# One expert's token gather in a mixture-of-experts step: tokens as the moving operand, 512 columns at a time, then transposed

## The chip, the cores and the metric

The kernel runs on one core of a Trainium2 chip. The metric is the device time of one execution in microseconds (us); the time before is the median of three runs. Engines are named as in the profile: PE is TensorE's matmuls and PEld its weight loads, DVE is VectorE, ACT is ScalarE, POOL is GpSimd, SP is the sync engine that issues the weight transfers.

## What is computed

One inference step of a two-layer decoder for 256 prompt tokens and 8 sample tokens (264 in all, width 1024). The last part, and the one that the change touches, is a mixture of 8 experts, each with an inner width of 3584; each token goes to its best two:

```python
logits = (h @ w_router).astype(jnp.float32) + b_router.astype(jnp.float32)
top_v, top_i = lax.top_k(logits, TOP_K)
gates = jax.nn.softmax(top_v, axis=-1)
...
for e in range(N_EXPERTS):
    y = (jax.nn.silu(h @ w1[e]) * (h @ w3[e])) @ w2[e]
    out = out + dense_gate[..., e:e + 1] * y
```

## The kernel before

Everything is float32 in memory. For the large products each operand is split into a high part, rounded to the format that PE streams quickly (F32R), and the remainder. A product is then three matmuls (`three`, L429 to L434): high by high, remainder by high, high by remainder.

**Weights.** An expert's weights come in 42 slabs of 1 MB (`eslabs`), through a ring of seven places filled by SP. For each slab ACT copies the high part (`high`, L1072, tile w_hi) and DVE subtracts it from the original (`low`, L1555, tile w_lo). There are three places for such pairs (`PAIRS`). ACT may write a place only when PE has used the slab that was in it three slabs before (semaphore `pair_used`); SP may refill a place of the ring only when DVE has made the remainder. The slabs of a chunk j of 512 inner channels are two of w1, two of w3, and two of w2 for the chunk before. The last two slabs of an expert are those of w2 for the last chunk, j = 6.

**An expert on PE** (`expert`): for each chunk, `product(1, j, 3)` and `product(3, j, 4)` multiply the gathered tokens (tiles xe_hi, xe_lo; 1024 channels in 8 blocks of 128, 128 token places) by w1 and w3, 24 matmuls of 512 columns each, 12 a slab. `turn(j)` transposes the activated product with four PE transposes (L814) into bank 5, ACT copies its high part (`turned_high`, L1086), DVE makes the remainder (`turned_low`, L1576), which sets `upT_ready`. `down(j)` then multiplies by w2 into banks 6 and 7, 12 matmuls a slab. `combine` scatters the former expert's result back by a matmul (L789), spread over the first chunks of the next expert.

**The gather** (`gather`, L771): for the next expert, while this one ends. `disp` holds 0/1 (which token goes to which of the 128 places), in three parts of 128, 128 and 8 tokens. For each of the 8 channel blocks of 128, the token rows (htok_hi, htok_lo) are the stationary operand and the 128 columns of disp stream: 8 blocks x 3 token parts x 2 (high, remainder) = 48 matmuls. The result in banks 0 and 1 has channels on partitions, as the products want it. Three more transposes (L777) turn the gated matrix. ACT copies the high part of both banks (`gathered_high`, L1077), DVE makes the remainder (`gathered_low`, L1560) and sets `xe_ready`, on which the next expert's first product waits.

**Order.** It is written out by hand for each engine, and each engine runs its list in order. PE at an expert's end: down(5), turn(6), gather, down(6), then the next expert's product(1, 0). In the program of ACT and of DVE one step of the loop over `eslabs` belongs to one slab k; it begins with `high` or `low` of slab k + 3, so with a wait for PE's use of slab k. In the step of (2, 5, 1) there follow turned_high or turned_low for chunk 6, and then gathered_high or gathered_low. The steps (2, 6, 0) and (2, 6, 1) hold only high or low. After the last step ACT copies half of the expert's result (L1103) and DVE the other half (L1601).

The first expert's gather has nothing around it; the next seven are issued in the expert before. The last expert issues none.

Of the kernel before, what the change touches and what calls it, by code (L numbers as in the profile page):

```python
# [9 lines left out]
ACT = mybir.ActivationFunctionType  # L10
# [66 lines left out]
def yoco_step(nc, w, o):  # L77
# [23 lines left out]
    with ExitStack() as ctx:  # L101
# [16 lines left out]
        def sem(name):  # L118
            return ctx.enter_context(nc.semaphore(name))
# [45 lines left out]
        def at(offset, *shape):  # L165
# [74 lines left out]
        ye = at(5632, D)  # L240
        disp = over("disp", "phase", 6656, [P, 3, SLOTS], F32R)
        dispg = at(7040, 3, SLOTS)
        comb = at(7424, NT)
        lg = at(7688, 3, NE)
        sel = at(7712, 3, NE)
# [47 lines left out]
        moe_ready, flag_ready = sem("moe_ready"), sem("flag_ready")  # L293
        route_built, gathered, comb_turned, comb_copied = (sem(n) for n in (
            "route_built", "gathered", "comb_turned", "comb_copied"))
        silu_done, up_ready, up_turned = (sem(n) for n in ("silu_done", "up_ready", "up_turned"))
        y0_copied, y1_copied, c_summed, y_added = (sem(n) for n in ("y0_copied", "y1_copied", "c_summed", "y_added"))
        y_turned, y_taken = sem("y_turned"), sem("y_taken")
# [127 lines left out]
        def _(pe):  # L426
# [331 lines left out]
            def gather(e, c, ahead):  # L758

                pe.wait_ge(route_built, e + (c * NE + ahead + 1))  # L760
                if ahead:

                    pe.wait_ge(y_added, e * KC + KC * (c * (NE + 1) + 1))
                elif c:
                    pe.wait_ge(y_added, KC * c * (NE + 1))
                pe.wait_ge(comb_copied, e + (c * (NE + 1) + ahead + 1))
                for k in range(KC):
                    for q in range(3):
                        n = rows[q]
                        for part, last in ((htok_hi, False), (htok_lo, q == 2)):  # L770
                            mm = pe.matmul(bank[k // 4][:, P * (k % 4):P * (k % 4) + SLOTS], part[0:n, q, P * k:P * (k + 1)], disp[0:n, q, :],  # L771
                                           start=(q == 0 and part is htok_hi), stop=last)
                    if k % 4 == 3:
                        mm.then_inc(gathered, 1)
                for q in range(3):
                    n = rows[q]
                    mm = pe.transpose(bank[2][0:SLOTS, P * q:P * q + n], dispg[0:n, q, :], ident[0:n, 0:n])  # L777
                mm.then_inc(comb_turned, 1)

            def combine(e, c, blocks=range(KC)):  # L780

# [10 lines left out]
            def expert(e, c, last):  # L792
# [21 lines left out]
                        mm = pe.transpose(bank[5][:, SLOTS * i:SLOTS * (i + 1)], up[0:SLOTS, P * i:P * (i + 1)], ident[0:SLOTS, 0:SLOTS])  # L814
                    mm.then_inc(up_turned, 1)

                def down(j):
                    pe.wait_ge(upT_ready, count(FCH, j + 2))
                    if j == 0:
                        pe.wait_ge(y0_copied, count(1, 1))  # L820
                        pe.wait_ge(y1_copied, count(1, 1))
                    for half in range(2):
                        hi, lo = weights(2, j, half, 2)
                        for i in range(2):
                            for q in range(2):
                                cols = slice(512 * q, 512 * (q + 1))
                                mm = three(bank[6 + q][0:SLOTS, :], (upT_hi[:, 2 * half + i, :], upT_lo[:, 2 * half + i, :]),
                                           (hi[:, i, cols], lo[:, i, cols]), j == 0 and half == 0 and i == 0, j == FCH - 1 and half == 1 and i == 1)
                        mm.then_inc(pair_used, 1)
# [15 lines left out]
                turn(FCH - 1)  # L845
                if not last:
                    gather(e, c, 1)
                down(FCH - 1)

            def experts(c):  # L850
                gather(0, c, 0)
                with pe.Fori(0, NE - 1) as e:
                    expert(e, c, False)
                expert(NE - 1, c, True)
                combine(NE, c)
# [18 lines left out]
        def _(act):  # L874
# [191 lines left out]
            def high(e, c, k):  # L1066
# [4 lines left out]
                    before_experts[slot] + 16 * ((c * NE + ahead) * len(use[slot]) + use[slot].index(k % PER_E) + 1)))  # L1071
                act.activation(w_hi[:, (NSPLIT + k) % PAIRS, :], ring[:, slot, :], ACT.Copy).then_inc(hi_done, 1)  # L1072

            def gathered_high(e, c, ahead):
                act.wait_ge(gathered, e * 2 + (2 * (c * NE + ahead) + 2))
                for q in range(2):
                    ins = act.activation(xe_hi[:, 4 * q:4 * q + 4, :], bank[q][:, :].rearrange("p (k n) -> p k n", k=4), ACT.Copy)  # L1077
                ins.then_inc(xe_hi_ready, 1)

            def expert(e, c, last):  # L1080
                def count(per, k):
                    return e * per + (c * NE * per + k)

                def turned_high(j):
                    act.wait_ge(up_turned, count(FCH, j + 1))
                    act.activation(upT_hi[:, :, :], bank[5][:, :].rearrange("p (k n) -> p k n", k=4), ACT.Copy).then_inc(upT_hi_ready, 1)  # L1086

                for k, (m, j, half) in enumerate(eslabs):

                    if k + PAIRS < PER_E or not last:  # L1090
                        high(e, c, k + PAIRS)
                    if (m, half) == (1, 1):
                        act.wait_ge(pair_used, used_by(e, c, 1, j))
                        act.wait_ge(up_ready, count(FCH, j + 1))
                        act.activation(up_s[0:SLOTS, :], bank[3][0:SLOTS, :], ACT.Silu).then_inc(silu_done, 1)
                        if j >= 1:
                            turned_high(j - 1)
                    if (m, j, half) == (2, FCH - 2, 1):
                        turned_high(FCH - 1)
                        if not last:  # L1100
                            gathered_high(e, c, 1)
                act.wait_ge(pair_used, used_by(e, c, 2, FCH - 1))
                act.activation(ye[0:SLOTS, 0:512], bank[6][0:SLOTS, :], ACT.Copy).then_inc(y0_copied, 1)  # L1103

            def experts(c):
                for k in range(PAIRS):
                    high(0, c, k)
                gathered_high(0, c, 0)
                with act.Fori(0, NE - 1) as e:
                    expert(e, c, False)  # L1110
                expert(NE - 1, c, True)
# [19 lines left out]
        def _(dve):  # L1131
# [420 lines left out]
            def low(e, c, k):  # L1552
                i, slot = (NSPLIT + k) % PAIRS, (NPRE + k) % RING
                dve.wait_ge(hi_done, e * PER_E + (NSPLIT + c * NE * PER_E + k + 1))
                dve.tensor_tensor(w_lo[:, i, :], ring[:, slot, :], w_hi[:, i, :].bitcast(F32), ALU.subtract).then_inc(lo_done, 1)  # L1555

            def gathered_low(e, c, ahead):
                dve.wait_ge(xe_hi_ready, e + (c * NE + ahead + 1))
                for q in range(2):
# [10 lines left out]
            def expert(e, c, last):  # L1570
# [8 lines left out]
                for k, (m, j, half) in enumerate(eslabs):  # L1579
# [16 lines left out]
                    if (m, j, half) == (2, FCH - 2, 1):  # L1596
                        turned_low(FCH - 1)
                        if not last:
                            gathered_low(e, c, 1)
                dve.wait_ge(pair_used, used_by(e, c, 2, FCH - 1))  # L1600
                dve.tensor_copy(ye[0:SLOTS, 512:1024], bank[7][0:SLOTS, :]).then_inc(y1_copied, 1)  # L1601

            def experts(c):
                route(0, c, 0)
                for k in range(PAIRS):
                    low(0, c, k)
                gathered_low(0, c, 0)
                with dve.Fori(0, NE - 1) as e:
                    expert(e, c, False)
# [119 lines left out]
```

## Time and profile before

| | |
|---|---|
| time before, median of 3 runs | 2040.87 us (2030.43 to 2042.6) |
| span of the profiled execution | 2030.6 us |
| PE busy | 1851.2 us, 91% |
| PEld busy | 1484.2 us, 73% |
| DVE busy | 1449.0 us, 71% |
| ACT busy | 1064.2 us, 52% |
| read from memory | 492 MB |
| mean granted TensorE clock | 0.889 |

The profiled execution's span is 0.2 us above the fastest of the three runs. Its total time is not told apart from its span. The experts run from 909 us to 2000 us. A matmul's duration in the trace includes its way through a pipeline, so that two neighbours overlap; what one costs PE is the distance from its start to the next one's. The granted clock is a share of full speed: 1.00 is 2.4 GHz and 0.50 is 1.2 GHz.

### The profile page before, as it was taken

What the parts mean: (1) busy time and instruction counts of PE and PEld (TensorE: products, weight loads), DVE (VectorE), ACT (ScalarE), POOL (GpSimd) and SP (SyncE); (2) the same over time, 40 slices, a digit from 0 to 9 for tenths busy, and PEclk for the clock granted to TensorE, in tenths of its full rate; (3) what the DMA queues carried; (4) which work ended last, traced back from release to release, by engine and by line L of the source; (5) the groups of instructions that cost most, each with busy time, mean ns of one, the idle gap of its engine ahead of it and who ended that gap; (6) DMA issues with size and microseconds to landing.
All of it is one profiled execution on the core that took longest, in us unless ns stands there. A gap on an engine that the chain in (4) does not pass through costs nothing.

```text
span 2030.6 us, 24253 instructions
## 1 busy us (share of the span) xinstructions
PE 1851.2 (91%) x9104; PEld 1484.2 (73%) x9104; DVE 1449.0 (71%) x1369; ACT 1064.2 (52%) x918; POOL 155.4 (8%) x113
## 2 busy tenths in 40 slices
PE   6567999788978999779999999999999999999995
PEld 2237999568953577547888888888888888888883
DVE  5965554677765464666879879878698698886883
ACT  5433433443311232535767767667577676675772
POOL 0430000200023242200000000000000000000000
PEclk9778999799976655868999999999899899998997
DMA  9744545564526510526989979969799799797980
GB/s 337 268 139 132 177 163 191 179 204 168 164 85 230 185 63 1 176 99 227 374 297 342 376 281 353 370 244 377 269 339 378 271 348 375 267 374 271 350 312 23
DMA packets 244290, 496.38 MB, mean 244 GB/s; under 512 B 9225, under 2 KB 68793, under 8 KB 244081
## 3 DMA queue, kind: packets, MB, share of 16 engines
q1 hardware_dynamic: 243243, 491.60, 68.4%
q0 software_dynamic: 640, 2.62, 0.3%
q10 hardware_dynamic: 334, 1.18, 0.2%
q8 instruction: 47, 0.77, 0.2%
q14 instruction: 26, 0.21, 0.0%
HBM read 492.03 MB, written 3.80 MB: 244 GB/s over the span
## 4 chain that ended last, share of the span: by engine, by line
PE 83%; DVE 11%; issue 2%; ACT 2%; POOL 1%; SPq 0%; DMA 0%; POOLq 0%; DVEq 0%; ACTq 0%
PE bank L432 21%; PE bank L433 21%; PE bank L434 21%; PE bank L771 4%; PE bank L677 3%; PE bank L495 2%; PE bank L789 2%; PE bank L655 2%; DVE w_lo L361 1%; PE bank L814 1%; DVE xT L1213 1%; PE bank L696 1%; DVE tT L1196 1%; ACT w_hi L892 1%; PE bank L482 1%
## 5 line engine op out<-in xcount | busy, mean ns | idle before, releaser
L1555 DVE TENSOR_TENSOR w_lo<-ring,w_hi 128x2048 fp32r<-128x2048 f32 x336 | 768.6, 2289 | 147.7 <-ACT w_hi L1072 147.0
L1072 ACT ACTIVATE w_hi<-ring 128x2048 fp32r<-128x2048 f32 x336 | 643.9, 1919 | 275.5 <-PE bank L434 275.4
L432 PE MATMUL bank<-w_hi,xe_hi 128*128 128x512 f32 x896 | 359.1, 401 | 1.9 <-DVE xe_lo L1560 1.9
L434 PE MATMUL bank<-w_hi,xe_lo 128*128 128x512 f32 x896 | 350.7, 391 | 0.0
L433 PE MATMUL bank<-w_lo,xe_hi 128*128 128x512 f32 x896 | 349.9, 391 | 0.0
L361 DVE TENSOR_TENSOR w_lo<-ring,w_hi 128x2048 fp32r<-128x2048 f32 (+1 forms) x90 | 208.2, 2321 | 146.4 <-ACT w_hi L892 144.0
L892 ACT ACTIVATE w_hi<-ring 128x2048 fp32r<-128x2048 f32 (+1 forms) x106 | 200.1, 1896 | 144.7 <-PE bank L434 71.7
L432 PE MATMUL bank<-tHi,w_hi 128*128 128x264 f32 x736 | 215.7, 293 | 22.3 <-DVE mLo L1273 20.4
L434 PE MATMUL bank<-tHi,w_lo 128*128 128x264 f32 x736 | 211.5, 287 | 0.0
L432 PEld LDWEIGHTS bank<-w_hi,xe_hi 128*128 128x128 f32 x896 | 169.0, 189 | 37.6 <-issue 1.9
L434 PEld LDWEIGHTS bank<-w_hi,xe_lo 128*128 128x128 f32 x896 | 168.7, 188 | 36.6
L433 PEld LDWEIGHTS bank<-w_lo,xe_hi 128*128 128x128 f32 x896 | 169.2, 189 | 34.1
L433 PE MATMUL bank<-mLo,w_hi 128*128 128x264 f32 x672 | 192.7, 287 | 0.0
L432 PE MATMUL bank<-w_hi,upT_hi 128*128 128x512 f32 x448 | 184.5, 412 | 1.8 <-DVE upT_lo L1576 1.8
L433 PE MATMUL bank<-w_lo,upT_hi 128*128 128x512 f32 x448 | 181.3, 405 | 0.0
L434 PE MATMUL bank<-w_hi,upT_lo 128*128 128x512 f32 x448 | 178.9, 399 | 0.0
L432 PEld LDWEIGHTS bank<-tHi,w_hi 128*128 128x128 f32 x736 | 141.9, 193 | 23.6 <-issue 23.1
L434 PEld LDWEIGHTS bank<-tHi,w_lo 128*128 128x128 f32 x736 | 141.3, 192 | 0.0
L433 PEld LDWEIGHTS bank<-mLo,w_hi 128*128 128x128 f32 x672 | 129.1, 192 | 0.5
L482 PE MATMUL bank<-w_hi,c 128*18 128x512 f32 x192 | 84.4, 440 | 37.1 <-DVE w_lo L361 23.5
L361 POOL TENSOR_TENSOR w_lo<-ring,w_hi 128x2048 fp32r<-128x2048 f32 x16 | 77.4, 4849 | 422.5 <-ACT w_hi L892 422.5
L432 PEld LDWEIGHTS bank<-w_hi,upT_hi 128*128 128x128 f32 x448 | 87.5, 195 | 22.0 <-DVE upT_lo L1576 2.0
(246 smaller groups left out, 2350.6 us busy)
## 6 DMA issues: line engine op xcount, KB each, us to landing
ring<-in_moe_w SPq DMA_DIRECT2D x336, 1024.0 KB, 6.6
ring<-in_ffn_w SPq DMA_DIRECT2D x30, 1024.0 KB, 5.3
ring<-in_ada_mix_w SPq DMA_DIRECT2D x24, 1024.0 KB, 7.8
ring<-in_ada_ffn_w SPq DMA_DIRECT2D x24, 1024.0 KB, 6.9
ring<-in_w_q SPq DMA_DIRECT2D x12, 1024.0 KB, 5.1
ring<-in_cache_k SPq DMA_DIRECT2D x24, 512.0 KB, 4.4
ring<-in_cache_v SPq DMA_DIRECT2D x24, 512.0 KB, 5.0
ring<-in_w_kv SPq DMA_DIRECT2D x8, 1024.0 KB, 5.3
```

The source lines that it names most:

```text
L361: eng.tensor_tensor(w_lo[:, i % PAIRS, 0:size], ring[:, n % RING, 0:size], w_hi[:, i % PAIRS, 0:size].bitcast(F32), ALU.subtract).then_inc ...
L432: pe.matmul(out, a[0], b[0], start=start, stop=False, skip_group_check=True)
L433: pe.matmul(out, a[0], b[1], start=False, stop=False, skip_group_check=True)
L434: return pe.matmul(out, a[1], b[0], start=False, stop=stop, skip_group_check=True)
L482: pe.matmul(out[0:18, :], c18[:, 4 * half + k, :], hi[:, k, :], start=(half == 0 and k == 0), stop=False, skip_group_check=True)
L495: mm = pe.matmul(bank[7][:, 0:NT], ones, tT[:, k, :], start=(k == 0), stop=(k == KC - 1))
L655: mm = pe.matmul(bank[2 * (b // 4) + q][32 * (b % 4):32 * (b % 4 + 1), :], s_pT[:, g, b, :], slab_view(n)[:, t % 2, 512 * q:512 * (q + 1)] ...
L677: mm = pe.matmul(b[:, 256 * (g % 2):256 * (g % 2) + n], qT[lo:lo + HD, g * KC + h // 2, c * P:(c + 1) * P], kT[lo:lo + HD, h // 2, 0:n], s ...
L771: mm = pe.matmul(bank[k // 4][:, P * (k % 4):P * (k % 4) + SLOTS], part[0:n, q, P * k:P * (k + 1)], disp[0:n, q, :], start=(q == 0 and par ...
L892: act.activation(w_hi[:, i % PAIRS, 0:size], ring[:, n % RING, 0:size], ACT.Copy).then_inc(hi_done, 1)
L1072: act.activation(w_hi[:, (NSPLIT + k) % PAIRS, :], ring[:, slot, :], ACT.Copy).then_inc(hi_done, 1)
L1555: dve.tensor_tensor(w_lo[:, i, :], ring[:, slot, :], w_hi[:, i, :].bitcast(F32), ALU.subtract).then_inc(lo_done, 1)
```

## The change

The stationary and the moving operand of the gather are exchanged. `disp` is stationary and 512 channels of the token rows stream, so that there are 2 halves x 3 token parts x 2 (high, remainder) = 12 matmuls, and the tokens come out as rows. A half in bank 0 is copied to the new tile x_rows by ACT (`rows_out`), the half in bank 1 by DVE (`moe_rows_out`). `turn_rows` then transposes them with 8 PE transposes back into banks 0 and 1, and from there gathered_high and gathered_low work as they did. x_rows lies in the tile `shared`, which nothing else uses in this stage. The last down-projection is split: its first slab comes before turn_rows and its second after. gathered_high and gathered_low move one step later, into the step of (2, 6, 0), behind high or low of that step.

```diff
@@ block.tensor, gather
-                for k in range(KC):
+                for half in range(2):
+                    cols = slice(512 * half, 512 * (half + 1))
                     for q in range(3):
                         n = rows[q]
                         for part, last in ((htok_hi, False), (htok_lo, q == 2)):
-                            mm = pe.matmul(bank[k // 4][:, P * (k % 4):P * (k % 4) + SLOTS], part[0:n, q, P * k:P * (k + 1)], disp[0:n, q, :],
+                            mm = pe.matmul(bank[half][0:SLOTS, :], disp[0:n, q, :], part[0:n, q, cols],
                                            start=(q == 0 and part is htok_hi), stop=last)
-                    if k % 4 == 3:
-                        mm.then_inc(gathered, 1)
+                    mm.then_inc(rows_gathered, 1)
...
+            def turn_rows(e, c, ahead):
+
+                for half, copied in enumerate((rows0_copied, rows1_copied)):
+                    pe.wait_ge(copied, e + (c * NE + ahead + 1))
+                    for k in range(4):
+                        mm = pe.transpose(bank[half][:, SLOTS * k:SLOTS * (k + 1)], x_rows[0:SLOTS, half, P * k:P * (k + 1)], ident[0:SLOTS, 0:SLOTS])
+                    mm.then_inc(gathered, 1)
...
                 turn(FCH - 1)
                 if not last:
                     gather(e, c, 1)
-                down(FCH - 1)
+                down(FCH - 1, (0,))
+                if not last:
+                    turn_rows(e, c, 1)
+                down(FCH - 1, (1,))
 
             def experts(c):
                 gather(0, c, 0)
+                turn_rows(0, c, 0)
...
@@ block.scalar
+            def rows_out(e, c, ahead):
+                act.wait_ge(rows_gathered, e * 2 + (2 * (c * NE + ahead) + 1))
+                act.activation(x_rows[0:SLOTS, 0, :], bank[0][0:SLOTS, :], ACT.Copy).then_inc(rows0_copied, 1)
...
                     if (m, j, half) == (2, FCH - 2, 1):
                         turned_high(FCH - 1)
                         if not last:
-                            gathered_high(e, c, 1)
+                            rows_out(e, c, 1)
+                    if (m, j, half) == (2, FCH - 1, 0) and not last:
+                        gathered_high(e, c, 1)
...
@@ block.vector
+            def moe_rows_out(e, c, ahead):
+                dve.wait_ge(rows_gathered, e * 2 + (2 * (c * NE + ahead) + 2))
+                dve.tensor_copy(x_rows[0:SLOTS, 1, :], bank[1][0:SLOTS, :]).then_inc(rows1_copied, 1)
...
                         turned_low(FCH - 1)
                         if not last:
-                            gathered_low(e, c, 1)
+                            moe_rows_out(e, c, 1)
+                    if (m, j, half) == (2, FCH - 1, 0) and not last:
+                        gathered_low(e, c, 1)
```

Ahead of the first expert, ACT runs rows_out before its gathered_high, and DVE runs moe_rows_out before its gathered_low, behind the three remainders that it makes there.

## Rows read from the trace of the kernel before

**Rows 1.** The page: the chain that ended last, by engine and by line.
```profile
PE 83%; DVE 11%; issue 2%; ACT 2%; POOL 1%; SPq 0%; DMA 0%; POOLq 0%; DVEq 0%; ACTq 0%
```
**Rows 2.** Waits, 930 to 1990 us: engine, line, what it waited for, total us, times, longest.
```profile
ACT w_hi L1072 <- PE bank L434: 275.4, 312, 5.2
...
ACT xe_hi L1077 <- PE bank L771: 53.9, 7, 9.0
...
PE bank L432 <- DVE upT_lo L1576: 1.8, 1, 1.8
```
**Rows 3.** Windows from turn(6) to the next expert's first product: length, busy, clock.
```profile
1043.95:1061.01 17.06, 17.06 (x80) 13.99 (x79) 6.52 (x6) 5.40 (x5) 0.00 (x0) 0.80 0.56 209
...
1309.94:1329.99 20.05, 20.05 (x80) 16.52 (x79) 6.54 (x6) 5.40 (x5) 0.00 (x0) 0.66 0.47 175
...
sum 129.93, PE 129.93 PEld 106.68 DVE 45.89 ACT 37.80 POOL 0.00; mean PE 18.56 PEld 15.24 DVE 6.56 ACT 5.40 POOL 0.00
```
**Rows 4.** Timeline of PE, 1176.5 to 1194.5 us: start, duration, instruction.
```profile
1176.45 0.39 PE L433 MATMUL bank<-w_lo,upT_hi 128*128 128x512 f32 x1
1176.68 0.40 PE L434 MATMUL bank<-w_hi,upT_lo 128*128 128x512 f32 x1
1176.92 0.60 PE L814 MATMUL bank<-const,phase 128*128 128x128 f32 x4
1177.28 0.31 PE L771 MATMUL bank<-disp,htok_hi 128*128 128x128 f32 x1
...
1178.21 0.33 PE L771 MATMUL bank<-disp,htok_hi 128*128 128x128 f32 x1
...
1185.88 0.89 PE L777 MATMUL bank<-const,phase 128*128 128x128 f32 x3
1186.70 0.80 PE L432 MATMUL bank<-w_hi,upT_hi 128*128 128x512 f32 x1
...
1194.04 0.39 PE L432 MATMUL bank<-w_hi,xe_hi 128*128 128x512 f32 x1
```
**Rows 5.** Timeline of ACT, then of DVE, the same stretch.
```profile
1177.12 1.91 ACT L1072 ACTIVATE w_hi<-ring 128x2048 fp32r<-128x2048 f32 x1 [0.83 <-PE bank L434]
...
1185.98 1.09 ACT L1077 ACTIVATE xe_hi<-bank 128x512 fp32r<-128x512 f32 x2 [6.47 <-PE bank L771]
...
1179.07 2.29 DVE L1555 TENSOR_TENSOR w_lo<-ring,w_hi 128x2048 fp32r<-128x2048 f32 x1 [0.41 <-ACT w_hi L1072]
1181.27 0.68 DVE L1576 TENSOR_TENSOR upT_lo<-bank,upT_hi 128x512 fp32r<-128x512 f32 x1
1187.10 1.29 DVE L1560 TENSOR_TENSOR xe_lo<-bank,xe_hi 128x512 fp32r<-128x512 f32 x2 [5.14 <-ACT xe_hi L1077]
```
**Rows 6.** Timeline of PE at the last expert's end, where no gather stands.
```profile
1984.86 0.60 PE L814 MATMUL bank<-const,phase 128*128 128x128 f32 x4
1987.26 0.50 PE L432 MATMUL bank<-w_hi,upT_hi 128*128 128x512 f32 x1 [1.80 <-DVE upT_lo L1576]
1987.60 0.39 PE L433 MATMUL bank<-w_lo,upT_hi 128*128 128x512 f32 x1
```
**Rows 7.** Windows around idle stretches of PE in earlier stages, columns as in rows 3.
```profile
298.30:300.60 2.30, 0.04 (x1) 0.07 (x1) 2.14 (x6) 1.82 (x3) 0.00 (x0) 1.00 0.91 287
300.60:304.00 3.40, 3.40 (x28) 3.40 (x29) 1.76 (x1) 0.32 (x1) 0.00 (x0) 1.00 0.13 42
384.70:387.30 2.60, 0.00 (x0) 0.00 (x0) 2.60 (x1) 1.93 (x2) 2.59 (x1) 1.00 0.00 0
...
388.20:391.20 3.00, 2.59 (x10) 0.91 (x7) 2.82 (x5) 0.92 (x2) 0.00 (x0) 0.50 0.87 279
...
483.80:487.20 3.40, 3.20 (x14) 3.23 (x15) 3.40 (x4) 0.00 (x0) 0.00 (x0) 0.50 0.00 0
487.20:490.00 2.80, 2.80 (x25) 2.80 (x24) 1.81 (x4) 0.00 (x0) 0.68 (x1) 1.00 0.56 170
```
**Rows 8.** Windows of the first gather, columns as in rows 3.
```profile
909.29:922.54 13.25, 13.25 (x48) 11.36 (x48) 6.32 (x3) 0.00 (x0) 0.00 (x0) 0.50 0.65 237
922.54:925.29 2.75, 0.89 (x4) 0.47 (x4) 1.29 (x2) 1.08 (x2) 0.00 (x0) 0.50 0.00 0
925.29:930.93 5.64, 5.64 (x13) 4.46 (x14) 0.00 (x0) 0.04 (x1) 0.00 (x0) 0.50 0.00 0
```
**Rows 9.** Windows of dense expert work, columns as in rows 3.
```profile
1061.00:1090.00 29.00, 29.00 (x131) 23.95 (x130) 25.84 (x21) 21.78 (x16) 0.00 (x0) 1.00 0.84 294
...
1167.00:1176.90 9.90, 9.90 (x45) 8.09 (x44) 8.76 (x7) 7.44 (x6) 0.00 (x0) 1.00 1.02 373
```

More of the change, by code:

```diff
@@ L242, in yoco_step @@
         dispg = at(7040, 3, SLOTS)
+        x_rows = shared[:, 0:D].rearrange("p (q n) -> p q n", q=2)
         comb = at(7424, NT)
@@ L295, in yoco_step @@
             "route_built", "gathered", "comb_turned", "comb_copied"))
+        rows_gathered, rows0_copied, rows1_copied = sem("rows_gathered"), sem("rows0_copied"), sem("rows1_copied")
         silu_done, up_ready, up_turned = (sem(n) for n in ("silu_done", "up_ready", "up_turned"))
@@ L815, in turn, with down @@
                     mm.then_inc(up_turned, 1)
-                def down(j):
+                def down(j, halves=(0, 1)):
                     pe.wait_ge(upT_ready, count(FCH, j + 2))
@@ L821, in down @@
                         pe.wait_ge(y1_copied, count(1, 1))
-                    for half in range(2):
+                    for half in halves:
                         hi, lo = weights(2, j, half, 2)
@@ L1107, in experts @@
                     high(0, c, k)
+                rows_out(0, c, 0)
                 gathered_high(0, c, 0)
@@ L1606, in experts @@
                     low(0, c, k)
+                moe_rows_out(0, c, 0)
                 gathered_low(0, c, 0)
```

## The prediction

> **What bounds the kernel now.** I read the page first, for the chain that ended last: 83% of it is PE [rows 1], so PE's time is the kernel's time unless something makes PE wait. Then the waits over the experts: ACT waits for PE 312 times, 275.4 us in all, DVE waits for ACT behind that, and nobody waits for a transfer. PE itself waits once, for 1.8 us [rows 2]. So in the experts what PE is given to do sets the time, and ACT, DVE and the ring follow it.
>
> Then PE's timeline at an expert's end. A matmul of 512 columns starts 0.23 us after the one before [rows 4], 0.229 us on the mean (12 of them a slab, 2.75 us). A gather block of six matmuls takes 1178.21 - 1177.28 = 0.93 to 0.96 us, about 0.16 us each, though each streams a quarter of the columns. And the gather ends in slower steps than it began: 1185.88 - 1177.28 = 8.6 us, where eight blocks at 0.96 would be 7.7. The windows say why: from turn(6) to the next expert's first product the granted clock is 0.66 to 0.80, while the dense work around it has 1.00 [rows 3, 9]. After the gather's thin stream the clock falls to its lower level (1.2 GHz), and the second half of the gather and the first matmuls of down(6) run at 0.43 us instead of 0.23. The seven stretches are 17.06 to 20.05 us long, 129.93 in all, mean 18.56 [rows 3]. The distance from a stretch's end to the next one's start (1061.01 to 1176.92 and 1194.04 to 1309.94) is 115.9 us every time. So a stretch's length after the change, minus 18.56, times seven, is most of the answer; the first gather is counted apart.
>
> **The change, part by part.** Time runs from the start of turn(6), at full clock.
>
> The gather on PE: removed are 48 matmuls at 0.16 us; added are 12 of 512 columns, 12 x 0.229 = 2.75, plus some 0.24 us a half for the entries to and from the 8-token part (in the block of six those two edges cost 0.20 instead of 0.11 us): 3.2 us. With turn (1177.28 - 1176.92 = 0.36) and the three L777 transposes (0.82 at half clock [rows 4], so about 0.45) PE would be ready for down(6) at 0.36 + 3.2 + 0.45 = 4.0.
>
> The Trainium skill has a rule that speaks against this part ("TensorE: Matmul & The Clock Gate", Back-to-back issue gap): an isolated matmul costs its columns at 2.4 GHz plus 2.5 ns, so 55.6 ns for 128 and 215.7 ns for 512. By it 48 small ones cost 2.7 us and 12 large ones 2.6, and nothing is gained. The trace agrees at 512 columns (0.23 us) and not at 128 (0.16 us); the same section says that this formula counts too little for short streams, since each has a weight load.
>
> The first new wait: upT_ready. ACT begins high of the next slab at 0.20 and takes 1.91 us, DVE starts low at 2.15 and takes 2.29, turned_low starts at 1181.27 - 1176.92 = 4.35 and takes 0.68: ready at 5.03 [rows 5]. Before, the gather covered this chain. Now PE arrives at 4.0 and waits about 1.1 us. The last expert, which has no gather, shows just such a wait: 1.80 us [rows 6]. So down(6)'s first slab starts at 5.08, and the gather's exact length on PE doesn't matter up to 1.1 us either way. rows_out (a copy like half of L1077, 0.55 us) runs at about 2.6 and moe_rows_out (0.68, as L1576) at about 5.0; both end before turn_rows needs them at 7.9, in time that the two engines idled before (6.47 and 5.14 us [rows 5]). If that cover were gone they would cost 0.7.
>
> The second new wait: xe_ready. First slab: 12 x 0.229 and 0.11 more behind a wait (1987.60 - 1987.26 = 0.34 against 0.23 [rows 6]) = 2.86, ending at 7.94. ACT's list now has high of the next slab before gathered_high, and that high waits for this slab: start 8.14, end 10.06; gathered_high (1.09) ends at about 11.1. On DVE, low of that slab must come first: 10.1 to 12.4; then gathered_low (1.29 [rows 5], the two nearly back to back) to 13.6. PE meanwhile does 8 transposes (two turns, 0.8 with their entry) and the second slab (2.75): done at 11.5. It waits 2.2 us and starts the next expert's product at 13.7; with the slow first matmul 13.8. Behind this wait on PE stands all of the next expert; on ACT and DVE the last high and low and the two result copies end by about 16.7, and combine wants them only at 13.8 + 5.5 = 19.3.
>
> The stretch: 5.08 + 2.86 + 5.8 = 13.8 us, so 7 x (18.56 - 13.8) = 33.3 us saved.
>
> The clock: the sparse stream that brought it down is gone, but two idle stretches of 1.1 and 2.2 us are new. An idle stretch of 2.3 us left the clock at 1.00, one of 2.6 us was followed by 0.50 from 388.20 on [rows 7]. The 2.2 us wait lies just under the two, so I expect it to fall sometimes. A fall costs what the stretch from 483.80 shows: 3.4 us at 0.50, then 1.00 again [rows 7]; in dense work those 3.4 us do eight matmuls where they would do fifteen, a loss of 1.6 us. I take two falls in seven, 3.2 us; the ends are none and seven (11 us).
>
> The first gather: now 13.25 us at 0.50, then 2.75 to the first product [rows 8]. After: 12 x 0.427 + 0.5 = 5.6 us at half clock. DVE's three remainders end at 915.6 (6.3 us of DVE in that window), 6.3 us after the gather's start; then its row copy 0.7, four transposes at half clock 0.9, gathered_high 1.1, gathered_low 1.3, edges 0.3: 10.6 us against 16.0, so 5.4 saved. If the clock rises during the now dense gather, up to 8 (part of the 5.64 us at 0.50 goes [rows 8]); if each edge costs more, 4.
>
> Transfers: no DMA is moved or added, SP's list is the same; slabs are requested as DVE makes remainders. An expert needs 42 MB (44.0 million bytes) in 115.9 + 13.8 = 129.7 us, 340 GB/s; dense stretches show 373 [rows 9]. Hidden.
>
> Sum: -33.3 + 3.2 - 5.4 = -35.5 us on the profiled execution's 2030.6, so 1995. The median of the runs is 10.3 us above that execution. Either those 10 us lie elsewhere and stay (2005), or they are longer gather stretches (seven at 20.05 instead of 18.56 would be 10.4 us) and go too (1995). I take the middle, 2000.
>
> **The rivals.**
> A, no new waits: PE's own work sets the stretch, 0.36 + 3.2 + 0.45 + 2.75 + 0.8 + 2.75 = 10.3; 7 x 8.3 + 5.4 = 63 us, so about 1973. For it speaks that PE almost never waits now [rows 2]; against it that the gather was what covered both chains, and [rows 6].
> B, the clock falls in nearly every stretch, at the second wait: seven falls cost 11 instead of 3.2: about 2008. It is the slow end of my forecast.
> C, slower than before: the clock falls already at the first wait or never recovers in the stretch. Then gather and turn take 6.8, the first slab 5.3, transposes and the second slab 6.7, and the next product starts at half clock for 1.6 more: 20.4, which is 1.8 us over 18.56; 7 x 1.8 - 5.4 = +7 us, about 2048. It decides where the stretch passes 18.56 + 0.8 us. Against it: what fed the fall was 8 us of thin stream, and dense matmuls now stand between the waits.
> D, the transfers become the bound: the pause in which the ring filled shrinks by 5 us. If they could hold no more than the 326 GB/s that an expert's 135 us now get, the period would stay and only the first gather's 5.4 us would come: 2035. For it: the DMA share is 1.02 in dense work [rows 9]. Against: ACT never waits for a slab [rows 2].
> E, the small matmuls cost nothing that large ones don't: the gather keeps its 7.7 us in 12 matmuls, PE is at down(6) at 8.5, and the stretch is 17.2; 7 x 1.4 saved: about 2031. That is what the skill's column formula would make of the exchange (no gain in it). 0.229 us for 512 columns stands against it.
>
> **How the numbers follow.** Forecast with two waits and few falls 0.58, A 0.09, B 0.14, C 0.04, D 0.06, E 0.02, others unseen 0.07. The forecast's own range is 1990 to 2010 (the 10 us of the median, first gather 4 to 8). For 8 in 10 it reaches toward A and past B: 1982 to 2022. A measurement of this kernel tells about 1% from no change, 20.4 us: faster takes the forecast, A, B and some of the unseen, 0.81; within 1% D, E, most of C and some of the unseen, 0.16; slower 0.03.
>
> **What would show it.** In the profile after: L771 x96 with 512 columns, starting 0.23 us apart; PE idle about 1.1 us before L432 on upT_lo and about 2.2 us before L432 on xe_lo, seven times each; the stretches 13.7 to 15.5 us long with the clock near 1.00 instead of 0.66 to 0.80; 115.9 us between them as before. I am wrong if the distance between stretches grows (transfers, DVE), if the clock in them stays at 0.8 or less, or if the waits are absent.

## The result

The changed kernel takes 2016.62 us (median of 4 runs, 2014.13 to 2018.28) against 2036.09 us for the kernel before (4 runs, 2030.43 to 2042.6). The ratio is 0.9903, 95% interval 0.9874 to 0.9933: faster by 1%, about 19 us. The forecast was 2000 us, 41 us under the 2040.87 us that the kernel before had in its first three runs; a fourth run brought that median to 2036.09. The profiled execution's span is 2015.6 us against 2030.6, so 15.0 us less where 35.5 were forecast. (A run's time is 1.8 us above its span: 2017.37 and 2015.6 us for the profiled run.)

The page of the changed kernel: the chain that ended last by engine, the granted clock in 40 slices.

```profile
PEclk9778999799975755968999999999999999999998
...
PE 80%; DVE 12%; issue 4%; ACT 3%; POOL 1%; SPq 0%; DMA 0%; POOLq 0%; DVEq 0%; ACTq 0%
```

PE still holds most of the chain, 80% where it was 83% [rows 1]; the shares of DVE, of ACT and of "issue" (time for which the profile shows no wait) have grown by one to two points each. The waits of the changed kernel's experts (PE's own, 900 to 2000 us) say where PE now stands still:

```profile
PE bank L434 <- DVE xe_lo L1585: 17.0, 8, 2.7
...
PE bank L434 <- DVE upT_lo L1601: 6.7, 8, 1.8
```

Both forecast waits are there, in all seven experts that gather (the eighth wait for xe_lo is the first gather's, the eighth for upT_lo the last expert's, as in [rows 6]). The timeline of one stretch, PE first, then ACT and DVE, answers to [rows 4, 5]:

```profile
1171.90 0.60 PE L824 MATMUL bank<-const,phase 128*128 128x128 f32 x4
1172.25 0.48 PE L774 MATMUL bank<-htok_hi,disp 128*128 128x512 f32 x1
1172.57 0.39 PE L774 MATMUL bank<-htok_lo,disp 128*128 128x512 f32 x1
...
1175.12 0.49 PE L774 MATMUL bank<-htok_hi,disp 8*128 8x512 f32 x1
...
1175.78 0.59 PE L779 MATMUL bank<-const,phase 128*128 128x128 f32 x3
1177.07 0.74 PE L434 MATMUL bank<-w_hi,upT_hi 128*128 128x512 f32 x1 [0.70 <-DVE upT_lo L1601]
1177.61 0.63 PE L435 MATMUL bank<-w_lo,upT_hi 128*128 128x512 f32 x1
1178.04 0.63 PE L436 MATMUL bank<-w_hi,upT_lo 128*128 128x512 f32 x1
...
1181.51 1.04 PE L787 MATMUL bank<-const,shared 128*128 128x128 f32 x8
...
1187.37 0.79 PE L434 MATMUL bank<-w_hi,xe_hi 128*128 128x512 f32 x1 [2.06 <-DVE xe_lo L1585]
```
```profile
1181.71 1.91 ACT L1086 ACTIVATE w_hi<-ring 128x2048 fp32r<-128x2048 f32 x1 [6.72 <-PE bank L436]
1183.52 1.07 ACT L1095 ACTIVATE xe_hi<-bank 128x512 fp32r<-128x512 f32 x2
...
1183.65 2.29 DVE L1576 TENSOR_TENSOR w_lo<-ring,w_hi 128x2048 fp32r<-128x2048 f32 x1 [6.12 <-ACT w_hi L1086]
1185.86 1.28 DVE L1585 TENSOR_TENSOR xe_lo<-bank,xe_hi 128x512 fp32r<-128x512 f32 x2
```

The gather takes 1175.78 - 1172.25 = 3.5 us instead of 8.6. PE waits 0.70 us for upT_lo and 2.06 for xe_lo, and xe_lo is late for the forecast reason: ACT and DVE first finish the next slab's pair. What was not forecast stands in the distances behind the waits: 1177.07 to 1177.61 to 1178.04 are 0.43 us and more. The clock is at its lower level behind both waits. The windows of the changed kernel (columns as in [rows 3]): a stretch and the sum of the seven, then the two pieces with the lower clock.

```profile
1171.90:1187.37 15.47, 12.71 (x52) 9.02 (x51) 8.79 (x8) 7.80 (x8) 0.00 (x0) 0.89 0.65 228
...
sum 108.20, PE 88.99 PEld 63.10 DVE 61.56 ACT 54.47 POOL 0.00; mean PE 12.71 PEld 9.01 DVE 8.79 ACT 7.78 POOL 0.00
```
```profile
1177.15:1180.55 3.40, 3.40 (x8) 2.68 (x9) 0.39 (x1) 0.00 (x0) 0.00 (x0) 0.50 1.05 392
1187.40:1190.80 3.40, 3.40 (x8) 2.72 (x9) 2.78 (x2) 0.34 (x1) 0.00 (x0) 0.50 0.77 294
1190.80:1200.00 9.20, 9.20 (x41) 7.56 (x41) 4.68 (x4) 7.88 (x6) 0.00 (x0) 1.00 0.41 134
```

Each piece holds 8 matmuls where 15 would fit: a loss of about 1.6 us. The seven stretches are 15.31 to 15.49 us long instead of 17.06 to 20.05. The second fall lies in the next expert, so the distance from a stretch's end to the next one's start is 117.6 us every time instead of 115.9.

The ledger against the spans: stretches 108.20 - 129.93 = -21.7; seven falls behind a stretch at 1.7 = +12 (six show as distances, the seventh as a clock of 0.50 from 1853.0 to 1856.4); the first gather -5.4 (below); together -15.1, measured 2015.6 - 2030.6 = -15.0.

The medians come from different comparisons, in which the kernel before took 2036.09 us here and about 2032 below; kernels of different comparisons are therefore set side by side by their ratios to it, or by the times inside their traces.

### The profile page after: what moved, and what is told of

Its sections match the earlier page's. It is cut to its first block, busy times and chain, and to the rows that moved or that the text cites. A ratio compares the mean times of both kernels' runs of the same rounds, so it can differ in the third digit from the quotient of the medians.

```text
span 2015.6 us, 23836 instructions
## 1 busy us (share of the span) xinstructions
PE 1816.2 (90%) x8880; PEld 1442.1 (72%) x8880; DVE 1453.1 (72%) x1377; ACT 1067.4 (53%) x926; POOL 155.6 (8%) x113
## 4 chain that ended last, share of the span: by engine, by line
PE 80%; DVE 12%; issue 4%; ACT 3%; POOL 1%; SPq 0%; DMA 0%; POOLq 0%; DVEq 0%; ACTq 0%
PE bank L434 21%; PE bank L435 21%; PE bank L436 21%; PE bank L679 3%; PE bank L497 2%; PE bank L799 2%; PE bank L657 2%; DVE w_lo L363 1%; ACT w_hi L1086 1%; DVE xT L1234 1%; PE bank L698 1%; PE bank L824 1%; DVE tT L1217 1%; ACT w_hi L906 1%; PE bank L484 1%
## 5 line engine op out<-in xcount | busy, mean ns | idle before, releaser
L434 PE MATMUL bank<-w_hi,xe_hi 128*128 128x512 f32 x896 | 364.3, 407 | 17.0 <-DVE xe_lo L1585 17.0
L435 PE MATMUL bank<-w_lo,xe_hi 128*128 128x512 f32 x896 | 354.3, 395 | 0.0
L435 PEld LDWEIGHTS bank<-mLo,w_hi 128*128 128x128 f32 x672 | 129.1, 192 | 0.5
```

The source lines that it names most:

```text
L434: pe.matmul(out, a[0], b[0], start=start, stop=False, skip_group_check=True)
L435: pe.matmul(out, a[0], b[1], start=False, stop=False, skip_group_check=True)
```

## The experiments

Theory: two chains of ACT and DVE make PE wait, and the clock falls at each wait. Rivals: the extra copies, transposes or transfers are what costs; the falls have another cause. All times are medians of the runs beside the kernel before, which took 2032 us (2031.66 to 2033.27) in these comparisons.

**Fill the waits, leave the chains.** A `filler(n)` of matmuls into bank 3, which nobody reads then:

```diff
+                if not last:
+                    filler(4)
                 down(FCH - 1, (0,))
                 if not last:
                     turn_rows(e, c, 1)
                 down(FCH - 1, (1,))
+                if not last:
+                    filler(9)
```

> The changed kernel with 4 matmuls of 512 columns more ahead of down(6) and 9 more behind it, into bank 3, which nobody reads then: PE works through its two waits without doing anything useful, and both chains stay as they are. Theory (the waits' idle time is what brings the clock down): the stretch keeps its two waits' length, but the clock stays at 1.00: 14 falls of 1.65 us go, stretch about 13.9 us, distance 115.9, span about 1993. Rival (the falls have another cause, the copies or the transposes or the 8-token matmuls): span 2015 or more, clock 0.89 in the stretch as now. Rival for the distance of 117.6 us (extra DVE and ACT work): distance stays.

Measured: 2001.74 us, ratio 0.9855 (0.9836 to 0.9874), span 1996.2. One stretch:

```profile
1298.51:1312.61 14.10, 14.09 (x65) 10.32 (x64) 8.79 (x8) 7.80 (x8) 0.00 (x0) 1.00 0.66 247
```

The clock is 1.00 in all seven, the distances are 116.0 us again. 13 matmuls an expert that compute nothing make the kernel faster, by 10 us going by the ratios to the kernel before (0.9855 against 0.9903), by 15 going by the medians, by 19 going by the profiled spans. So the falls come from what PE does around the waits, and the longer distance was the clock and not copies or transfers: they are unchanged here.

**Take away the second wait.** gathered_high and gathered_low ahead of high and low in the step of (2, 6, 0). ACT's half of the edit; DVE's is alike:

```diff
+                    if (m, j, half) == (2, FCH - 1, 0) and not last:
+                        gathered_high(e, c, 1)
                     if k + PAIRS < PER_E or not last:
                         high(e, c, k + PAIRS)
...
-                    if (m, j, half) == (2, FCH - 1, 0) and not last:
-                        gathered_high(e, c, 1)
```

> In the step of (2, 6, 0), gathered_high and gathered_low stand ahead of high and low instead of behind them; nothing else. Theory (two chains of ACT and DVE make PE wait, and the TensorE clock falls at each wait): xe_ready then comes about 2.5 us after turn_rows, before the second slab of down(6) is through, so the 2.06 us wait goes (a stretch of 13.3 us instead of 15.5) and with it the fall of the clock at the start of the next expert, so that the distance between stretches is 115.9 us again and not 117.6. Seven times 3.9 us: a span of about 1988 us against 2015.6. Rival 1 (the longer distance is the extra copies on DVE and ACT, or the transfers): only the 2.2 us go, distance stays 117.6, span about 2000. Rival 2 (the late high and low of the next slab become the next wait): span about 2015.

Measured: 1987.55 us, ratio 0.9789 (0.9768 to 0.9811). The wait and its fall are gone (distances 116.0). The stretches are shorter than the theory said, because the fall at the first wait came in two of seven only; one with and one without:

```profile
1040.71:1054.01 13.30, 12.60 (x53) 9.04 (x51) 6.52 (x6) 5.52 (x6) 0.00 (x0) 0.87 0.79 283
1170.03:1181.78 11.75, 11.05 (x52) 7.87 (x51) 6.53 (x6) 5.52 (x6) 0.00 (x0) 1.00 0.79 293
```

**Take away the first wait.** turned_high and turned_low ahead of high and low in the step of (2, 5, 1), in the same manner.

> In the step of (2, 5, 1), turned_high and turned_low stand ahead of high and low; nothing else. Theory: upT_ready comes at about 1.8 us of the stretch, PE goes from the gather straight to down(6), the 0.9 us wait and the fall of the clock that begins there go: seven times 2.6 us, span about 1997. Rival (the clock falls there for the gather itself, whose 8-token matmuls fill few rows, and for the transposes, not for the wait): the wait goes, the clock still falls: seven times 1.0 us, span about 2009.

Measured: 1998.07 us, ratio 0.9839 (0.9816 to 0.9863). Stretches 12.96 to 13.14 us with the clock at 1.00, as the theory had it. But the second wait, still there and 2.1 us long, was now followed by a fall in two of seven (distances 116.0 four times, 117.6 twice). So a wait by itself doesn't decide. Nor do the gather's 8-row matmuls by themselves, the rival's case: they are all there, PE doesn't wait behind them, and no fall comes there in any of the seven. The next three runs ask what decides.

**Shift the period.** In the changed kernel every expert takes 133.1 us, and in all seven the falls begin at nearly the same places, 5.2 to 5.5 us and 15.5 to 15.7 us after the stretch's start. Four matmuls more in an expert's dense part:

```diff
+                    if j == 3:
+                        pe.wait_ge(comb_copied, e + (c * (NE + 1) + 2))
+                        for i in range(4):
+                            pe.matmul(bank[2][0:SLOTS, :], htok_hi[:, i % 2, 0:SLOTS], htok_hi[:, i % 2, 0:512], start=True, stop=True)
```

> The changed kernel with 4 matmuls of 512 columns more in the dense part of each expert (chunk 3, into bank 2, which nobody reads then), 0.9 us of work an expert, 6 to 7 us in all. In the changed kernel each expert takes 133.07 us and the clock falls at the same two places in all seven. Theory A (whether a wait of 1 or 2 us brings the clock down depends on when it comes, and the experts' equal period makes all seven alike): with the period shifted the falls differ from expert to expert, fewer than 14, and the span is 2015.6 + 6.4 less 1.65 us for each fall that goes, about 2012. Theory B (these waits always bring it down): 14 falls again, 2022.

Measured: 2016.37 us, ratio 0.9919 (0.9896 to 0.9943), so 7 us more work for the same time. Two stretches of the seven:

```profile
1044.62:1058.52 13.90, 11.14 (x52) 7.86 (x51) 8.80 (x8) 7.80 (x8) 0.00 (x0) 1.00 0.69 251
1177.07:1192.37 15.30, 12.53 (x53) 8.92 (x51) 8.82 (x8) 7.82 (x8) 0.00 (x0) 0.89 0.62 229
```

The waits are the same in both. The first wait brought a fall in three of seven, the second in five: 8 falls for 14. Theory A stands as far as that the same wait brings a fall or none by when it comes. Its sum said a span of 2012, and 2018.5 was measured. The experts lost and gained as it said (from the first stretch's start to the last one's end 809.6 us, against 813.8 in the changed kernel, with about 6 us more work), but the profiled execution came to its first stretch 5.8 us later, at 1044.6 instead of 1038.8. The traces show where: 5.0 of the 5.8 us stand ahead of the first gather (914.56 against 909.55 us), in stages that the edit doesn't touch. Over the eleven traces the first gather starts between 909.1 and 914.6 us; what moves it is not shown, and no difference of a few microseconds between two single spans should be read as the edit's.

**Full rows in the gather.** What else is around the first wait? The third token part has 8 rows of 128:

```diff
-                        n = rows[q]
                         for part, last in ((htok_hi, False), (htok_lo, q == 2)):
-                            mm = pe.matmul(bank[half][0:SLOTS, :], disp[0:n, q, :], part[0:n, q, cols],
+                            mm = pe.matmul(bank[half][0:SLOTS, :], disp[:, q % 2, :], part[:, q % 2, cols],
```

> The changed kernel with the third token part of the gather replaced by the first part over again, 128 rows instead of 8 (the 8 sample tokens are left out of the experts and the first 128 counted twice; as many matmuls, the same columns, the same copies). Theory (the wait brings the clock down): the gather is 0.5 us shorter, the chains and both waits stay, the clock falls at both: span 2015. Rival (the 8-row matmuls ahead of the wait are part of it): the fall at the first wait goes, seven times 1.6 us, span about 2004.

Measured: 1998.96 us, ratio 0.9827 (0.981 to 0.9843). The stretches are 13.74 to 13.92 us with the clock at 1.00: no fall at the first wait in any. And that wait is longer than in the changed kernel (waits of the experts):

```profile
PE bank L434 <- DVE upT_lo L1600: 10.1, 7, 1.4
```

That is what the rival forecast: without 8-row matmuls ahead of it, a wait twice as long brought no fall. The second wait, 2.06 us as before, was followed by a fall in one of the seven (distance 117.6 once, 116.0 otherwise), so the span, 1999.4 us, is below the rival's 2004. It also shows that equal periods (129.9 us here) don't make seven experts one and the same case, as the next expectation still has it. The run was repeated with the four matmuls of the shift:

> full_rows with the same 4 matmuls more an expert as shift_4 (the 8 sample tokens are left out, the first 128 counted twice). Without the shift, the clock never fell at the first wait though PE waited 1.4 us there, longer than in the changed kernel; but with an equal period all seven experts are one and the same case. With the shift they come at different times. Theory (the 8-row matmuls ahead of the wait are part of what brings the clock down): no fall at the first wait in any of the seven. Rival (only the time at which the wait comes counts): falls at it in about three of seven, as in shift_4.

Measured: 2013.41 us (2 runs), ratio 0.9908 (0.9877 to 0.9938). Clock 1.00 in all seven stretches, of which one:

```profile
1173.99:1187.90 13.91, 10.40 (x52) 8.18 (x51) 8.81 (x8) 7.81 (x8) 0.00 (x0) 1.00 0.76 273
```

The distances are 116.9 us three times and 118.5 three times: with the period shifted the second wait brought a fall in four of seven, the first in none. Falls at an expert's end, for every run of the new gather in which PE waits there:

| run | PE's first wait (rows of the last gather matmuls; three transposes stand between) | falls there | second wait | falls there |
|---|---|---|---|---|
| changed kernel | 0.70 us (8 rows) | 7 of 7 | 2.06 us | 7 of 7 |
| shift_4 | 0.70 us (8 rows) | 3 of 7 | 2.06 us | 5 of 7 |
| xe_first | 0.70 us (8 rows) | 2 of 7 | none | |
| up_first | none (8 rows) | 0 of 7 | 2.06 us | 2 of 7 |
| no_split (below) | 0.64 us (8 rows) | 0 of 7 | none | |
| full_rows | 1.45 us (128 rows) | 0 of 7 | 2.06 us | 1 of 7 |
| full_rows_shift | 1.45 us (128 rows) | 0 of 7 | 2.06 us | 4 of 7 |

With 8-row matmuls ahead, a first wait of 0.6 to 0.7 us was followed by a fall in 12 of 28 cases; with 128-row matmuls, one twice as long in 0 of 14. Without the changed kernel, whose seven are alike, that is 5 of 21 against 0 of 14: it speaks for a part of the 8-row matmuls in the first fall, but it is few cases. For the second wait they are not needed: dense 128-row matmuls stand right ahead of it in every run.

**Was it the exchange?** The kernel before with its old gather of 48 matmuls, cut in two halves around down(6)'s first slab, gathered_high and gathered_low one step later:

```diff
                 if not last:
-                    gather(e, c, 1)
-                down(FCH - 1)
+                    gather(e, c, 1, range(KC // 2))
+                down(FCH - 1, (0,))
+                if not last:
+                    gather(e, c, 1, range(KC // 2, KC))
+                down(FCH - 1, (1,))
```

> The kernel before, its gather unchanged (48 matmuls of 128 columns), but in two halves: blocks 0 to 3, first slab of down(6), blocks 4 to 7, second slab; gathered_high and gathered_low one step later. Theory (the long thin stream brings the clock down, and of the old stretch's 18.6 us only part is the gather's own work): PE works 0.4 + 3.85 + 3.85 + 0.4 + 5.5 us and waits 0.9 us for upT_ready, so a stretch of 14.9 us without falls, 16.5 with one: a span of 2005 without and 2016 with. Rival (what counts is the 48 matmuls, not the clock): seven times nothing, 2031.

Measured: 2036.52 us (10 runs, 2020.78 to 2052.37), ratio 1.0016 (0.998 to 1.0052): no gain, and a wide scatter. The rival's number came, but not its reason: in the theory's sum a stretch has 14.9 us of work and waits, and the one with a single fall of 3.4 us took 16.75, the others, with 6.8 to 13.7 us at the lower clock, up to 20.52. The theory erred by its clock: it allowed one fall at most.

```profile
1178.26:1195.01 16.75, 15.81 (x81) 12.95 (x80) 8.22 (x6) 5.40 (x5) 0.00 (x0) 0.90 0.65 233
...
1446.43:1466.95 20.52, 19.96 (x81) 15.96 (x80) 8.21 (x6) 5.39 (x5) 0.00 (x0) 0.67 0.66 238
```

In the last four of the seven the clock falls 3.6 to 3.7 us after the stretch's start, inside the first half and before PE has waited: half of the thin stream is enough there. In the first three it falls only behind the new wait of 0.94 us. Placed like this, the old gather gains nothing. A third of its matmuls has 8 rows too, and no run takes these out of it, so how much of the falls is due to the narrow columns and how much to the few rows isn't shown.

**Without the split.** gather, turn_rows, then both slabs of down(6); gathered_high and gathered_low directly behind the row copies, so ahead of the next slab's high and low. PE's part of the edit:

```diff
                     gather(e, c, 1)
-                down(FCH - 1, (0,))
-                if not last:
                     turn_rows(e, c, 1)
-                down(FCH - 1, (1,))
+                down(FCH - 1)
```

> The changed kernel with the last down-projection whole again: gather, turn_rows, then both slabs of down(6); gathered_high and gathered_low directly behind the row copies. Theory: PE waits once, about 1.3 us between gather and turn_rows for DVE's row copy, which stands behind low and turned_low; all 24 matmuls then cover the xe chain, so the second wait and its fall of the clock go. Stretch 11.9 us plus 1.6 for a fall at the first wait: span about 1990. Rival (the split is what hides the row copies and so carries the gain): copies and transposes show on PE, span 2015 or more.

Measured: 1983.48 us, ratio 0.976 (0.9744 to 0.9776), so faster than the split kernel by 29 to 33 us (by the ratios, by the medians). PE's only wait in the stretch, 0.6 us each time, is now for DVE's row copy, and no fall followed it in any of the seven; the stretches are 11.7 us. The rival, that the split carries the gain, is wrong. How much comes from the whole down-projection and how much from gathered_high and gathered_low standing ahead of the next slab's pair isn't told apart: the second alone (xe_first) was worth 23 to 29 us.

```profile
PE bank L787 <- DVE shared L1577: 4.5, 7, 0.6
```

**Both reorderings together**, split kept.

> Both reorderings together. Theory: no wait and no fall at an expert's end, stretch about 12.4 us or less, clock 1.00 in it, distance 115.9: seven times 6.5 us, span about 1970, 3% under before. Rival (gather itself brings the clock down): one fall of 1.6 us an expert stays, span about 1982. Rival (ACT and DVE have no slack left, new waits for w_lo): over 1985.

Measured: 1979.45 us (1976.58 to 1980.6), ratio 0.974 (0.972 to 0.9761), the fastest kernel of the study. A stretch, and its timeline on ACT and DVE:

```profile
1168.97:1179.96 10.99, 10.99 (x53) 7.87 (x51) 6.53 (x6) 5.52 (x6) 0.00 (x0) 1.00 0.96 352
```
```profile
1169.61 0.60 ACT L1104 ACTIVATE upT_hi<-bank 128x512 fp32r<-128x512 f32 x1 [1.27 <-PE bank L824]
1170.11 1.91 ACT L1086 ACTIVATE w_hi<-ring 128x2048 fp32r<-128x2048 f32 x1
...
1177.32 1.09 ACT L1095 ACTIVATE xe_hi<-bank 128x512 fp32r<-128x512 f32 x2 [4.83 <-PE bank L787]
...
1178.44 1.29 DVE L1585 TENSOR_TENSOR xe_lo<-bank,xe_hi 128x512 fp32r<-128x512 f32 x2 [3.50 <-ACT xe_hi L1095]
1180.24 2.29 DVE L1576 TENSOR_TENSOR w_lo<-ring,w_hi 128x2048 fp32r<-128x2048 f32 x1 [0.52 <-ACT w_hi L1086]
```

xe_lo is ready at 1179.73, 0.2 us before PE gets to it, and PE works through the stretch without a wait. Its span, 1977.8 us, is 8 us above the forecast 1970, though stretch and distance (116.0) are as short as said or shorter. 3 us of it lie ahead of the first gather (912.79 against 909.55 us in the changed kernel), another 3 in the optimism of seven times 6.5 (15.47 - 10.99 + 1.6 = 6.1), and the fall behind the last stretch gave nothing back: from that stretch's end to the end of the execution it is 162.8 us here and 163.0 there.

## Why the prediction was right and where it was wrong

**Right: what bounds it.** PE's time, ended by stretches between constant distances. Without a fall in it such a distance was 115.9 to 116.0 us, before and after, and 116.9 in the two runs with four matmuls more. The prediction named a growing distance as a sign of being wrong. It grew, to 117.6 us, but neither by transfers nor by DVE: it is the second wait's fall, and fill_both has 116.0 again.

**Right: the two chains.** Forecast 13.8 us for a stretch at full clock. No stretch of the changed kernel was at full clock, but shift_4 has four, with the same instructions: 13.90. The parts: first slab at 5.08, measured 1177.07 - 1171.90 = 5.17; waits 1.1 and 2.2, measured 0.70 and 2.06, which the profile counts from the modelled end of the last matmul, 0.1 to 0.2 us after its successor could have started; gather 3.2, measured 3.5. The timeline shows why: behind every change between 128 and 8 rows two starts in a row are late, 0.31 to 0.34 us apart instead of 0.23, so a change costs 0.2 us and not the 0.1 that the sum has. full_rows, with no such change, does its gather in 1174.30 - 1171.46 = 2.8 us. As the prediction said, the gather's exact length is hidden in the first wait, which is shorter by as much.

**Right in sum, by two errors that cancel: the first gather.** Forecast -5.4. Windows of the changed kernel, which answer to [rows 8]:

```profile
909.55:915.83 6.28, 6.28 (x12) 3.29 (x12) 6.28 (x3) 0.60 (x1) 0.00 (x0) 0.50 0.52 166
915.83:921.30 5.47, 2.79 (x13) 2.04 (x12) 2.05 (x4) 1.09 (x2) 0.00 (x0) 0.50 0.98 348
921.30:924.56 3.26, 3.26 (x8) 2.58 (x9) 0.00 (x0) 0.00 (x0) 0.00 (x0) 0.50 0.15 62
```

11.75 us to the first product instead of 16.00, so 4.25 where the forecast had 10.6 us and 5.4; and 3.26 us at half clock behind it instead of 5.64, worth another 1.2, which the -5.4 didn't count. That they make 5.4 together is luck.

**Right: transfers are hidden** (rival D). The waits name no slab, and xe_first and no_split run the same transfers in 29 and 33 us less than the changed kernel.

**Wrong: the number of falls.** The step that failed is "I take two falls in seven, 3.2 us". Its price was right, 1.6 us each; its count was 2 where 14 came. 12 x 1.6 = 19 us is nearly all of the 20.5 us between the forecast -35.5 and the measured -15.0 on the profiled execution. So 2016.62 us lies above the forecast's own range of 1990 to 2010, and inside 1982 to 2022 only because that range reached past rival B. Two errors are in the step. For the second wait the step looked at the idle time alone, between one of 2.3 us without and one of 2.6 us with a fall [rows 7]; the same 2.1 us are followed by a fall in 7, 5, 4, 2 or 1 of seven experts, depending on the run, so the idle time alone doesn't give a count, and the two in seven of the forecast would have been right for up_first. What made all seven alike in the changed kernel isn't shown: its experts come 133.1 us apart, those of up_first come 129.1 apart when no fall lies between, just as evenly, and there two of seven fell. For the first wait the step counted nothing; rival C names a fall there and sets against it that the thin stream is gone and dense matmuls stand between the waits. By columns the new gather is dense, but a third of its matmuls, the last two among them, use 8 of 128 rows, and behind those a wait of 0.7 us was followed by a fall in 12 of 21 cases, if never behind the 0.64 us of no_split.

**Rivals B and C.** B named seven falls at the second wait and 2008 us; the case that came is B with the first wait's falls as well, 2016.6. C named a fall at the first wait, but let the clock stay down for the whole stretch; it was back after 3.4 us each time.

**Rival E, and what made the gather shorter.** 12 streams of 512 columns took 3.5 us at full clock, where 48 of 128 would have taken 7.7 (eight blocks of 0.96), so the exchange did gain on PE. But the 0.16 us that the prediction has for a small matmul is a mean of two costs. The kernel before, at full clock:

```profile
1177.42 0.28 PE L771 MATMUL bank<-disp,htok_lo 128*128 128x128 f32 x1
1177.53 0.28 PE L771 MATMUL bank<-disp,htok_hi 128*128 128x128 f32 x1
1177.64 0.27 PE L771 MATMUL bank<-disp,htok_lo 128*128 128x128 f32 x1
1177.84 0.32 PE L771 MATMUL bank<-disp,htok_hi 8*128 8x128 f32 x1
1178.01 0.27 PE L771 MATMUL bank<-disp,htok_lo 8*128 8x128 f32 x1
```

Starts are 0.11 us apart where the rows stay 128, and 0.16 to 0.20 behind a change of rows, which the old gather has 15 times and the new one 3 times. An estimate from these starts: 48 small matmuls at 0.11 would take 5.3 us, against 2.7 us for 12 large ones at 0.229, so of the 4.2 us gained some 2.5 are due to the wider stream and some 1.6 to the fewer changes of rows. No run has the old gather with its 8-row matmuls grouped, which would test it.

The rule of columns at 2.4 GHz plus 2.5 ns stands in the Trainium skill ("TensorE: Matmul & The Clock Gate", Back-to-back issue gap), which itself says that it counts too little for short streams. At 128 columns this trace disagrees with the rule even where no rows change: 0.11 us, about twice its value.

**The 10 us between the runs.** The forecast left open whether they lie in the gather stretches. 1.8 us of the 10.3 are no difference between runs at all: the text set a median of run times against a span. The kernel before in later comparisons ran at 2027.0 to 2040.8, median 2032; the changed one ran four times, within 2014.1 to 2018.3. That would fit if stretches of 17.1 to 20.1 us by chance of the clock were part of the scatter, but four runs don't show it, and up to 5 us of what differs between traces lies ahead of the first gather.

## What to carry to other kernels

When work is taken out of the bounding engine, look in the orders of the other engines for what that work had covered: here two chains that began with a slab's copy which nobody was in a hurry for. Putting the short step for which PE waits ahead of the long one that has three slabs of time (both_first) was worth 33 to 37 us (by ratios, by medians), more than the change itself. And reckon with a clock fall at each new wait, even one of 0.7 us, up to one in every turn of the loop: the second wait, 2.06 us long, had 7 falls of 7 in the changed kernel and 1 of 7 in full_rows, though both loops run with equal periods.

## What the runs showed of the hardware

- Waits of 0.70 us (behind 8-row matmuls) and 2.06 us were each followed by 3.4 us at 1.2 GHz, 14 times of 14 in the changed kernel; the same waits in shift_4 8 times of 14.
- The first wait behind matmuls of 128 rows, twice as long (1.45 us), 0 times of 14 (full_rows, full_rows_shift); a wait of 0.64 us behind 8-row matmuls 0 times of 7 (no_split). Why is not shown.
- In the kernel before and in before_spread the clock fell while PE streamed 128-column matmuls, a third of them with 8 rows, without a wait, 3.3 to 6.7 us after the stretch's start in the former.
- 13 matmuls an expert that compute nothing made the kernel faster: 2001.74 us (ratio 0.9855) instead of 2016.62 (0.9903).
- After a change between 128 and 8 rows, in either direction, the next two starts are late: at 512 columns by about 0.1 us each (0.31 to 0.34 us apart instead of 0.23).
- Full-row matmuls of 128 columns, each with a new stationary operand, start 0.11 us apart at full clock, those of 512 columns 0.23.
